# A chunked delta rule's triangular inverse: products of levels 4, 8 and 16 as four 32x32 blocks in place of two 64x64

## What is computed

```
def step(state, inp):
    r_t, w_t, k_t, v_t, kk_t, a_t = inp
    sk = jnp.einsum('bhvk,bhk->bhv', state, kk_t)
    state = (state * w_t[:, :, None, :]
             - sk[..., None] * (kk_t * a_t)[:, :, None, :]
             + v_t[..., None] * k_t[:, :, None, :])
    y = jnp.einsum('bhvk,bhk->bhv', state, r_t)
    return state, y
```

## Time and profile before

| | |
|---|---|
| runs | 1702.53, 1705.26, 1707.93 us (median 1705.26) |
| span of the profiled execution | 1704.8 us |
| busy | PE 96%, weight loads 73%, DVE 51%, ACT and POOL 41% |
| level products, group 0 and 1 | about 282 to 309 us and 348 to 377 us |
| wu and parts, group 0 and 1 | about 309 to 322 us and 377 to 391 us |
| mean granted clock of TensorE | 0.986 of full |

### The profile page before, as it was taken

How to read it: one execution, slowest core, us unless ns; L and a number is a source line. 1 busy time by engine, 2 the same in 40 slices (tenths; PEclk the granted TensorE clock), 3 DMA queues, 4 the chain that set the end, 5 groups by cost and what they waited for, 6 DMA issues and landing times. The chain is left out here.

```text
span 1704.8 us, 25057 instructions
## 1 busy us (share of the span) xinstructions
PE 1634.1 (96%) x10298; PEld 1251.2 (73%) x10298; DVE 872.5 (51%) x1464; ACT 692.2 (41%) x1184; POOL 702.8 (41%) x353
## 2 busy tenths in 40 slices
PE   6999999798899899999999999999999999999999
PEld 5866667797787587888888888566677577777787
DVE  5947876445932435543331139497635564224252
ACT  5444453323532543222233233333655456355441
POOL 4533335033644044555554445444133412463343
PEclk9999999899999999999999999999999999999999
DMA  5421111003423022333323334111111310442132
GB/s 179 135 77 56 50 57 45 3 4 113 136 87 99 13 87 76 98 99 99 94 86 102 102 99 142 50 50 62 50 50 56 111 50 25 131 161 91 50 94 80
DMA packets 39569, 138.54 MB, mean 81 GB/s; under 512 B 4384, under 2 KB 5664, under 8 KB 38304
## 3 DMA queue, kind: packets, MB, share of 16 engines
q1 hardware_dynamic: 39456, 136.94, 25.3%
HBM read 132.73 MB, written 4.19 MB: 80 GB/s over the span
## 5 line engine op out<-in xcount | busy, mean ns | idle before, releaser
L388 POOL TENSOR_TENSOR parts<-ring,parts 128x1024 fp32r<-128x1024 f32 (+3 forms) x250 | 578.5, 2319 | 819.2 <-ACT parts L379 819.0
L426 PE MATMUL banks<-h_hi,parts 128*128 128x512 f32 x1120 | 466.4, 416 | 4.4 <-PEq L293 4.4
L428 PE MATMUL banks<-h_hi,parts 128*128 128x512 f32 x1120 | 442.8, 395 | 0.0
L427 PE MATMUL banks<-h_lo,parts 128*128 128x512 f32 x1120 | 442.6, 395 | 0.0
L379 ACT CAST parts<-ring 128x1024 fp32r<-128x1024 f32 (+3 forms) x251 | 244.9, 978 | 148.0 <-PE banks L428 148.0
L426 PEld LDWEIGHTS banks<-h_hi,parts 128*128 128x128 f32 x1120 | 211.8, 189 | 68.9 <-issue 21.2
L427 PEld LDWEIGHTS banks<-h_lo,parts 128*128 128x128 f32 x1120 | 212.0, 189 | 49.8 <-issue 4.9
L428 PEld LDWEIGHTS banks<-h_hi,parts 128*128 128x128 f32 x1120 | 211.5, 189 | 49.5
L3018 ACT CAST ffn_act_hi<-ffn_gate 128x512 fp32r<-128x512 f32 x22 | 13.7, 621 | 168.0 <-DVE ffn_gate L2917 168.0
L2974 DVE TENSOR_TENSOR ffn_raw<-banks,ffn_root 128x512 f32<-128x512 f32 x22 | 15.2, 691 | 125.7 <-PE banks L428 125.6
L428 PE MATMUL banks<-ffn_act_hi,parts 128*128 128x512 f32 x176 | 68.5, 389 | 0.0
(11 more groups left out here) (593 smaller groups left out, 2963.0 us busy)
## 6 DMA issues: line engine op xcount, KB each, us to landing
ring<-weights SPq DMA_DIRECT2D x211, 512.0 KB, 3.5
ring<-weights SPq DMA_DIRECT2D x24, 256.0 KB, 2.6
ring<-weights SPq DMA_DIRECT2D x8, 384.0 KB, 3.1
x<-xT SPq DMA_DIRECT2D x2, 1024.0 KB, 6.5
x<-xT SPq DMA_DIRECT2D x1, 2048.0 KB, 7.6
x_spill<-x SPq DMA_DIRECT2D x2, 1024.0 KB, 4.8
x<-x_spill SPq DMA_DIRECT2D x1, 2048.0 KB, 9.5
outT<-x SPq DMA_DIRECT2D x8, 256.0 KB, 2.0
```

Of the source, the lines that this page charges most:

```text
L388: self.nc.gpsimd.tensor_tensor(self.parts[:, t % PARTS, 1, 0:w], self.ring[:, t % SLOTS, 0:w], self.parts[:, t % PARTS, 0, 0:w].bitcast(F3 ...
L426: nc.tensor.matmul(out, w.hi, x.hi, start=first, stop=False)
L427: nc.tensor.matmul(out, w.hi, x.lo, start=False, stop=False)
L428: return nc.tensor.matmul(out, w.lo, x.hi, start=False, stop=last)
```

## The change

`pe_cx` and `pe_xcx` loop over a list of blocks where they looped over the two halves of the partitions. For level index 0 (size 2) and for size 32 the list is the two halves as before. For the sizes 4, 8 and 16, where the matrices and their products are zero outside the diagonal 32x32 blocks, the list has four entries of 32 rows and the 32 columns of the same block. The copies and subtractions still take whole banks; the parts of a bank outside the diagonal blocks keep what the product of level 2 wrote there. Nothing else changes.

```
+BLOCK = 32
...
+    def blocks(i):
+
+        if i == 0 or 2 * LEVELS[i] > BLOCK:
+            return [(rows, slice(0, CH)) for rows in HALF]
+        return [(slice(at, at + BLOCK), slice(at % CH, at % CH + BLOCK)) for at in range(0, P, BLOCK)]
...
@@ pe_cx
-                for c in range(2):
-                    last = nc.tensor.matmul(lane.units[lane.cx][HALF[c], e, u, :], quad(lane.part[i % 2], c, e, u),
-                                            quad(lane.inv, c, e, u), start=True, stop=True)
+                for rows, cols in blocks(i):
+                    last = nc.tensor.matmul(lane.units[lane.cx][rows, e, u, cols], lane.part[i % 2][rows, e, u, cols],
+                                            lane.inv[rows, e, u, cols], start=True, stop=True)
...
@@ pe_xcx
-                    for c in range(2):
-                        last = nc.tensor.matmul(lane.units[bank][HALF[c], e, u, :], quad(left, c, e, u), quad(right, c, e, u),
+                    for rows, cols in blocks(i):
+                        last = nc.tensor.matmul(lane.units[bank][rows, e, u, cols], left[rows, e, u, cols], right[rows, e, u, cols],
                                                 start=True, stop=True)
```

## The result

The changed kernel takes 1739.11 us (median of 5 runs, 1734.7 to 1743.56) against 1704.17 us for the kernel before (5 runs): a ratio of 1.0203, 95% interval 1.0186 to 1.022. It is slower by 35 us. The profiled execution took 1739.35 us, with a span of 1737.5 against 1704.8.

What follows compares the result with a forecast made beforehand. The prediction took TensorE's instruction supply, just above the levels' pace, as the limit the change would cross. Instructions +27.7, waits +2 and clock +3 gave +32.7 us, a span of 1737.5 and a median of 1738 us, range 1726 to 1747.

Steps and rivals of the forecast that it cites:

- The bound: Levels: TensorE busy throughout at 68 instructions per us, just under an instruction supply limit of 71 per us.
- The 3.55 us behind the 71: TensorE's instruction queue: fastest supply is one block of 251 instructions per 3.55 us; bounds 3.25 and 3.65.
- Array time: Changed levels: a product takes 0.47 to 0.94 us of array instead of 0.935; does not enter the sum.
- Instructions: Changed levels through parts: 768 instead of 384 instructions per level costs +14.4 us in group 0, +13.3 in group 1, together +27.7.
- Waits: TensorE's wait for ACT's copy ahead of each lane's parts delays entry into a block: +1 us per group, +2 in all.
- Clock: TensorE waiting for blocks falls to half clock, so unchanged level 32 could start slow: +1.5 us per group, +3.
- The sum: Whole kernel: 27.7 + 2 + 3 = +32.7 us on the profiled span of 1704.8, giving 1737.5.
- (a): Rival: supply is not the limit, levels take 3.5 to 4 us set by the chain; faster, 1693 us; chance 0.11.
- (b): Rival: each record costs 14.7 ns and instructions arrive in time, so no change, 1705 us; chance 0.04.
- (c): Rival: half clock through level 32, wu and the recurrence's start; each group loses another 3 to 4 us, 1745; chance 0.15.
- (d): Rival: supply limit with look-ahead, the next block asked for earlier, 3.3 us per block, 1731 us; chance 0.10.

Runs made afterwards that it cites:

- e3: Kernel before, with the 64x64 matmuls of the parts issued a second time, 1536 more instructions and no new tile: 1728.72 us, ratio 1.0127.
- e5: Changed kernel with the products of levels 4, 8 and 16 made for one head of each pair only: 1707.28 us, ratio 1.0011 to the kernel before.
- e7: Kernel before, with 32x32 blocks at levels 4, 8 and 16 for one head of each pair only: 1719.3 us, ratio 1.0074.
- e2: Kernel before, with 32x32 blocks at level 4 alone: 1719.26 us, ratio 1.0077.
- e1: Changed kernel with tiles of 64 rows by 32 columns at the three levels, as many instructions: 1739.62 us, ratio 1.0194 to the kernel before.
- e4: Kernel before (64x64 tiles), products of levels 4, 8 and 16 made for one head of each pair only: 1689.62 us, ratio 0.9904.
- e6: Changed kernel plus an unused full-width matmul behind each update product at the changed levels: 1741.99 us, ratio 1.0211 to the kernel before.

## Why the prediction was right

**The bound.** The prediction said that the levels run just under a limit of supply, 71 instructions per us, and that the change would cross it. e3, e5 and e7 bear this out, e3 with nothing changed but the number of instructions. The 3.55 us behind the 71 is not what the rows give, though: the prediction calls it the mean of the two stops, but their packets start 3.6 us (318.1 to 321.7) and 3.7 us (386.5 to 390.2) apart, 3.65 on average, which is its upper bound. With 3.65 the sum would have been 2.7 us higher. The changed kernel's packets came every 3.47 us in group 0 and 3.66 in group 1, so that 3.55 lies between them is in part luck, and the ceiling is no sharp figure: 256 instructions in 3.47 to 3.9 us are 74 to 66 per us.

**Array time** (0.47 to 0.94 us per product, with no part in the sum). At full clock the first products in e2 and in the changed kernel follow one another by 0.60 us, at half clock by 0.87 (290.00 to 290.87 for one whole product in the changed kernel). So at full clock the blocks do work faster on the array than the 0.935 us of before, by a third, and what is saved there is lost in stops; at half clock, where the changed levels mostly ran, the gain is small.

**Instructions** (+27.7 us for both groups). Group 0 took +16.2 us in all, of which 1.8 are level 32's half clock: 14.4, and 14.4 were predicted. Group 1 ran from 370.3 to 422.6 us, 52.3 against 34.8, of which level 32 took 6.11 us instead of 3.75. That leaves 15.1 against 13.3, as its blocks came every 3.66 us. Together 29.5, where the count and the waits below had 29.7. A level of group 0 took 9.3 us, then 10.6 and 10.4; the first as a block was in hand. The packets, 91, are as many as counted. The stops were shorter than the 2.5 us foretold, 1.5 us on average (27.7 us in 18), and the longest was 2.2.

**Waits** (+2). No run shows this term. The waits for ACT's copies are 0.70 and 0.78 us in each group as before, and what they delay cannot be told from what the supply did: wu and parts took 14.0 us instead of 13.0 in group 0, and 13.1 instead of 13.5 in group 1.

**Clock** (+3). It fell as expected, for most of the changed levels: 0.56 on average in both groups. Level 32 behind them took 1.8 us more in group 0 and 2.4 in group 1, 4.2 in all. I had put 3. How much of the 4.2 reached the whole time is not shown: a block can arrive during a slow level 32, and in e1, at full clock, level 32 had a stop by "issue" of 0.86 us of its own.

The sum, +32.7 on the profiled span, was met by +32.7. That it agrees to the tenth is luck: the two groups took 33.6 us more, the stretch between them 1.3 more and the rest 0.4 more, the start of group 0's levels came 2.6 us earlier in the profiled execution, and the executions of one kernel differ by 5 us and more.

The rivals: (a), a hidden supply, fell with e3 and e5. Its chain was about right, though: where supply was no limit, e4's levels, whose products take the 0.47 us that (a) supposed, lasted 3.2 us, just under its 3.5 to 4. The changed kernel's own products take 0.60, and no run shows them without the supply limit. (b), no gain on the array and no change, is excluded by the measured time; its 14.7 ns a record were 9.4 at full clock. (c) named an effect that exists, but its size in e2 and in the changed kernel is 1.1 to 2.4 us per group, not 3 to 4 more. (d) had blocks every 3.3 us; the mean intervals were 3.47 and 3.66 and, in e3, 3.5.

The sentence of the Trainium skill ("Runtime: NRT & Kernel Launch", section "Instruction fetch mechanics") that crossing a 16 KiB boundary is "mostly hidden" does not hold for this stage: group 0's three changed levels alone have 13.3 us of stops at such borders. It fits the stages of the kernel before where instructions are few: at 800 us its matmuls of 512 moving columns start 0.23 us apart, and there is no stop by "issue" between them.

What stays open: why the blocks came every 3.9 us in e1 and every 3.5 in e3 and in group 0 of the changed kernel. The trace of e1 shows where the time lies, between TensorE's resuming and the start of the next packet, 1.5 to 1.6 us in place of some 1.1, but not what causes it. The pace of the array at full clock is nearly the same in e1 and e3 (some 14.5 ns a record), and no run tells them apart. The single longer gaps in the changed kernel are not explained either.

## What to carry to other kernels

Count instructions per microsecond beside busy time: here a float32 matmul is four instructions on TensorE, and stretches that asked for more than about 70 per us stopped every 256 of them, on 64x64, 64x32 and 32x32 tiles alike. Splitting small matmuls into smaller ones pays only as far as the instruction stream has room, and this unrolled stage of 64x64 matmuls in float32, at 68 per us, had almost none. The sign in a profile is an idle time put down to "issue" inside a run of like matmuls, with a packet of the instruction queue that starts 2.2 to 2.8 us ahead of its end.

## What was not expected

- One changed level is enough for the next to start at half clock (e2): TensorE busy 4.8 of 10.5 us, then 6.8 us for an unchanged level instead of 5.65. In e7, whose levels have shorter stops, the clock stayed at 2.4 GHz.
- Matmuls put in to fill the stops filled them only in part (e6): 15.1 us of them took 5.2 us off the stops and made group 0's levels 7.9 us longer.
- Blocks came every 3.9 us in e1 at full clock, slower than the 3.47 us in group 0 of the changed kernel, mostly at half clock.
